# The quads of further expert blocks laid between the experts' own quads, in a kernel of two model blocks on one core

## The reference

```python
def hier_moe(h, router_g, router_g_b, router_e, router_e_b, w_gate, w_up, w_down):
    # top-1 of 4 expert groups, then top-2 of its 8 experts, gate = p(group) * renormalised p(expert | group)
    ...
    for gi in range(N_EXPERT_GROUPS):
        hid = jax.nn.silu(jnp.einsum('td,edf->tef', xt, w_gate[gi])) * jnp.einsum('td,edf->tef', xt, w_up[gi])
        hid = hid * gates[:, gi, :, None].astype(hid.dtype)
        out = out + jnp.einsum('tef,efd->td', hid, w_down[gi]).astype(f32)
```

## Time and profile before

| | us |
|---|---|
| median of 3 runs (3490.64 to 3506.99) | 3491.89 |
| the profiled execution: its own time | 3489.51 |
| the profiled execution: span from first to last instruction | 3487.7 |
| PE busy | 3098.4 |
| DVE busy | 1413.7 |
| ACT busy | 1080.6 |
| POOL busy | 310.3 |

### The profile page before, as it was taken

How to read it: one execution, slowest core, us unless ns; L and a number is a source line. 1 busy time by engine, 2 the same in 40 slices (tenths; PEclk the granted TensorE clock), 3 DMA queues, 4 the chain that set the end, 5 groups by cost and what they waited for, 6 DMA issues and landing times. The chain is left out here.

```text
span 3487.7 us, 54795 instructions
## 1 busy us (share of the span) xinstructions
PE 3098.4 (89%) x24140; PEld 2389.4 (69%) x24140; DVE 1413.7 (41%) x2665; ACT 1080.6 (31%) x1725; POOL 310.3 (9%) x460
## 2 busy tenths in 40 slices
PE   6888886888899788879999898999899998898998
PEld 5777765333788653337777676777687876777998
DVE  5455565211444641143333334333433334435554
ACT  4344443111443321133222213222332223224443
POOL 0122220111000011200000110000000000000000
PEclk9898898999999999989999899999999999999999
DMA  6333234788665169853443323453222222203452
GB/s 257 123 108 130 105 129 189 319 348 338 250 219 213 44 272 383 351 224 142 162 162 142 125 85 133 151 191 136 79 97 91 97 91 91 92 30 113 158 185 102
DMA packets 113629, 580.06 MB, mean 166 GB/s; under 512 B 24048, under 2 KB 26608, under 8 KB 60400
## 3 DMA queue, kind: packets, MB, share of 16 engines
q1 hardware_dynamic: 66160, 449.96, 34.2%
q0 software_dynamic: 47232, 126.60, 10.1%
HBM read 669.79 MB, written 1.05 MB: 192 GB/s over the span
## 5 line engine op out<-in xcount | busy, mean ns | idle before, releaser
L352 PE MATMUL ps<-t,t 128*128 128x512 f32 (+1 forms) x3488 | 1222.8, 351 | 114.3 <-DVE t L546 53.2
L353 PE MATMUL ps<-t,t 128*128 128x512 f32 (+1 forms) x3488 | 1211.7, 347 | 0.0
L354 PE MATMUL ps<-t,t 128*128 128x512 f32 (+1 forms) x3488 | 1210.2, 347 | 0.0
L329 DVE TENSOR_TENSOR t<-t,t 128x1024 fp32r<-128x1024 f32 x448 | 550.4, 1232 | 778.5 <-ACT t L310 778.4
L352 PEld LDWEIGHTS ps<-t,t 128*128 128x128 f32 x3488 | 668.2, 192 | 223.4 <-issue 69.6
L354 PEld LDWEIGHTS ps<-t,t 128*128 128x128 f32 x3488 | 668.3, 192 | 85.8
L353 PEld LDWEIGHTS ps<-t,t 128*128 128x128 f32 x3488 | 669.1, 192 | 82.0
L310 ACT ACTIVATE t<-t 128x1024 fp32r<-128x1024 f32 x448 | 469.6, 1054 | 589.1 <-PE ps L354 580.4
L1357 PE MATMUL ps<-t,t 128*32 128x512 f32 x1504 | 229.7, 638 | 46.2 <-DMA t<-in_experts_dram,t 35.9
L684 POOL DMA_DIRECT2D t<-in_wmod_dram x224 | 118.7, 535 | 1186.5 <-PE ps L633 1043.2
L1357 PEld LDWEIGHTS ps<-t,t 128*32 128x32 f32 x1504 | 52.4, 115 | 187.7 <-issue 99.4
(11 more groups left out here) (309 smaller groups left out, 2974.9 us busy)
## 6 DMA issues: line engine op xcount, KB each, us to landing
t<-in_wall_dram SPq DMA_DIRECT2D x221, 1024.0 KB
t<-in_experts_dram SPq DMA_DIRECT2D x192, 1024.0 KB, 6.5
t<-in_wmod_dram POOLq DMA_DIRECT2D x224, 512.0 KB, 5.7
t<-in_wmod_dram SPq DMA_DIRECT2D x16, 512.0 KB, 13.5
t<-in_wall_dram SPq DMA_DIRECT2D x10, 512.0 KB
t<-in_lora_dram POOLq DMA_DIRECT2D x8, 512.0 KB, 3.8
t<-in_rcst_dram POOLq DMA_DIRECT2D x1, 1536.0 KB, 6.3
t<-in_experts_dram,t POOLq DMA_INDIRECT x90, 5.6
```

The lines of the kernel that those rows point to most:

```text
L329: e.tensor_tensor(lo, self.raw(n), hi, ALU.subtract).then_inc(*net.wlo.up((self.name, n)))
L352: e.matmul(out, lh, rh, start=start, stop=False, **kw)
L353: e.matmul(out, lh, rl, start=False, stop=False, **kw)
L354: return e.matmul(out, ll, rh, start=False, stop=stop, **kw)
```

## The change

The further quads stand at turns 1, 4, 7 and 10 (`ORDER`). A method `turns` writes one list of steps, and all engines and the table of slots go by it. In each group of three turns A, O, B (O is the further quad) the steps that read weights stand as A0, O0, down of the previous B, A1, O1, B0, down A, down O, B1: two steps of the experts' own blocks stand between any two steps of the further quads, except for one at the very start. The further quads have four rooms of their own from the beginning (`far_rooms`), their own PSUM bank for gate up (3), their own gathered tokens (`Ug[1]`, gathered for two further quads at a time) and matrix `G[1]`; `hT` is doubled, and `S` has three buffers. In the first layer GpSimd clears the four rooms, which nothing has written before. The core of the diff:

```diff
-    ORDER = (0, 1, 8, 2, 3, 9, 4, 5, 10, 6, 11, 7)
+    ORDER = (0, 8, 1, 2, 9, 3, 4, 10, 5, 6, 11, 7)
...
-        self.S = [net.rview(256) for _ in range(2)]
-        self.sg, self.h, self.hT = f(256), f(256), f(256)
+        self.S = [net.rview(256), net.rview(256), net.take(256, R, at=net.nt_at + 256)]
+        self.sg, self.h, self.hT = f(256), f(256), [f(256), net.nt[0]]
...
-        first = [x for x in range(8) if net.turn[NS + x] < 0]
-        drawn = (first + [x for x in range(8) if x not in first])[0:4]
-        self.router = None
+        first = sum(net.turn[NS + x] < 0 for x in range(4, 8))
+        self.far_rooms = more[0:4]
+        net.fewer_rooms(range(4))
+        self.router, near = None, 0
...
-                if near == NS + MORE - 1:
-                    net.fewer_rooms(drawn)
                 if x >= 32:
-                    self.w[n, t, s] = net.drawn_slot(drawn[t], more[drawn[t]], ("block", x - 32, s), net.sums, key)
+                    self.w[n, t, s] = net.drawn_slot(t, more[t], ("block", x - 32, s), net.sums, key)
...
+    def turns(self):
+        out = []
+        for j in range(5):
+            A, O, B = 3 * j, 3 * j + 1, 3 * j + 2
+            if j < 4:
+                out += [("gate up", A, 0)]
+            if j == 0:
+                out += [("gather", 4, 0, 1), ("gather", 4, 1, 2)]
+            if j < 4:
+                out += [("gate up", O, 0)]
+            if j:
+                out += [("down", B - 3)]
+            if j == 4:
+                return out + [("scatter", B - 3)]
+            out += [("gate up", A, 1)]
+            if j:
+                out += [("scatter", B - 3)]
+            else:
+                out += [("gather", 4, 2, 1), ("gather", 4, 3, 2)]
+            out += [("turn", A, 0), ("gate up", O, 1), ("gate up", B, 0), ("turn", O, 3)]
+            if j < 3:
+                out += [("gather", j + 1, 0, 1), ("down", A), ("gather", j + 1, 1, 3), ("scatter", A), ("down", O), ("gate up", B, 1)]
+                out += [("scatter", O), ("turn", B, 0), ("gather", j + 1, 2, 1), ("gather", j + 1, 3, 2)]
+                if j == 1:
+                    out += [("gather", 5, kk, (3, 1, 2, 3)[kk]) for kk in range(4)]
+                continue
...
-        b = self.take(w, 0, "gate up", n) if s == 0 else self.bank("gate up", n)
+        b = self.take(w, 3 if n % 3 == 1 else 0, "gate up", n) if s == 0 else self.bank("gate up", n)
...
-        if g > 1:
-            w.wait_ge(*self.of(net.sums, "weights", 2 * g - 3, 1))
+        if g % 4:
+            w.wait_ge(*self.of(net.sums, "weights", self.members(g - 1)[1], kk // 2))
...
     def pool_blocks(self, e, w):
         net = self.net
+        if self.l == 0:
+            for x in range(4):
+                m = e.memset(self.far_rooms[x], 0.0)
+            m.then_inc(*self.up(net.pools, "rooms cleared"))
+            w.wait_ge(*self.of(net.pools, "rooms cleared"))
         w.wait_ge(*self.of(net.vecs, "block experts"))
...
-                    w.wait_ge(*marks.of(key))
+                    if freed is not None:
+                        w.wait_ge(*freed[0].of(freed[1]))
```

More of the change, by code:

```diff
@@ L830, in drawn_slot @@
         i, room = len(self.slots), NS + x
-        self.slots.append((room, ap, self.drawn[x], SW, what, self.freed[room], None))
+        self.slots.append((room, ap, self.drawn[x], SW, what, self.freed.get(room), None))
         self.drawn[x] += 1
@@ L1299, in __init__, with place, members @@
                     near += 1
-        net.fewer_rooms([x for x in range(MORE) if x not in drawn])
+        net.fewer_rooms(range(4, MORE))
         self.mods_rooms = [net.freed[NS + x] for x in range(8, MORE)]
+    def turns(self):
[23 more added lines that the diff above has]
+                    out += [("gather", 5, kk, (3, 1, 2, 3)[kk]) for kk in range(4)]
+                continue
+            pair = lambda what, x: [(what, x), (what, x + 1)] if self.ctx else []
+            out += pair("square", 0) + [("down", A)] + pair("ctx", 0) + [("scatter", A)] + pair("square", 2) + [("down", O)]
+            out += pair("ctx", 2) + [("gate up", B, 1)] + pair("square", 4) + [("scatter", O)] + pair("ctx", 4)
+            out += pair("square", 6) + [("turn", B, 0)] + pair("ctx", 6)
+    def place(self, n):
+        j, x = divmod(n, 3)
+        return (4 + j // 2, j % 2) if x == 1 else (j, x // 2)
+    def members(self, g):
+        return (3 * g, 3 * g + 2) if g < 4 else (6 * g - 23, 6 * g - 20)
     def blocks(self, n):
@@ L1447, in pe @@
         self.pe_spread(e, w)
-        for n in range(self.QUADS):
-            g, kk = n // 2 + 1, 2 * (n % 2)
-            self.pe_gate_up(e, w, n, 0)
-            if n:
-                self.pe_down(e, w, n - 1)
-            if g < 6:
-                self.pe_gather(e, w, g, kk, 3)
-            if n:
-                self.pe_scatter(e, w, n - 1)
-            if g == 6 and self.ctx:
-                for c in (2 * kk, 2 * kk + 1):
-                    self.ctx().pe_square(e, w, c)
-            self.pe_gate_up(e, w, n, 1)
-            if g < 6:
-                self.pe_gather(e, w, g, kk + 1, 1)
-            elif self.ctx:
-                for c in (2 * kk + 2, 2 * kk + 3):
-                    self.ctx().pe_square(e, w, c)
-            self.pe_turn(e, w, n, 3 if g < 6 else 0)
-        self.pe_down(e, w, self.QUADS - 1)
-        self.pe_scatter(e, w, self.QUADS - 1)
+        for what, n, *more in self.turns():
+            if what == "gate up":
+                self.pe_gate_up(e, w, n, *more)
+            elif what == "gather":
+                self.pe_gather(e, w, n, *more)
+            elif what == "turn":
+                self.pe_turn(e, w, n, *more)
+            elif what == "down":
+                self.pe_down(e, w, n)
+            elif what == "scatter":
+                self.pe_scatter(e, w, n)
+            elif what == "ctx":
+                self.ctx().pe_square(e, w, n)
         for o in range(7):
@@ L1721, in dve @@
         net.bg_dve.go(e, w, 2)
-        self.dve_choice(e, w, 1)
+        self.dve_choice(e, w, 4)
         self.dve_slots(e, w, 0)
-        for n in range(self.QUADS):
-            r = self.rows(n)
-            if n:
-                self.dve_down(e, w, n - 1)
-            w.wait_ge(*self.of(net.acts, "silu", n))
-            w.wait_ge(*self.of(net.vecs, "slot gate", n))
-            if n:
-                w.wait_ge(*self.of(net.sums, "turn", n - 1))
-            e.scalar_tensor_tensor(out=self.h[r, :], in0=self.sg[r, :], scalar=self.gs[r, n % 2:n % 2 + 1],
-                                   in1=net.ps[r, self.bank("gate up", n), 256:512], op0=ALU.mult, op1=ALU.mult).then_inc(
-                *self.up(net.vecs, "hidden", n))
-            self.emptied(net.vecs, ("hidden", n), "gate up", n)
-            if n % 2 and n < 9:
-                self.dve_choice(e, w, (n + 3) // 2)
+        for what, n, *more in self.turns():
+            if what == "down":
+                self.dve_down(e, w, n)
+            if what != "gate up" or more[0] == 0:
+                continue
+            self.dve_hidden(e, w, n)
+            if n % 3 == 0 and n < 9:
+                self.dve_choice(e, w, n // 3 + 1)
+            if n == 4:
+                self.dve_choice(e, w, 5)
             if n + 1 < self.QUADS:
                 self.dve_slots(e, w, n + 1)
-        self.dve_down(e, w, self.QUADS - 1)
         for o in range(8):
```

109 lines of the change are left out of this document (63 added, 46 removed).

## The result

| | before | changed |
|---|---|---|
| median, us | 3491.26 (4 runs, 3489.77 to 3506.99) | 3441.45 (4 runs, 3438.54 to 3446.89) |
| the profiled execution: its own time, us | 3489.51 | 3438.54 |
| first layer, first gate up step to last scatter, us | 270.3 | 243.0 |
| second layer, us | 264.9 | 244.1 |
| from the first layer's end to the second's start, us | 378.3 | 378.3 |

The ratio of the changed kernel's time to that of the kernel before is 0.9844, with a 95% interval of 0.9817 to 0.987: faster, by 1.6%. The prediction was 3439 us for the median.

What follows compares the result with a forecast made beforehand. TensorE and SyncE's fetch queue were taken to idle in turn, waiting on further fetches that move almost nothing. 3489.5 - 59.8 + 7 = 3436.7, with 2.4 to the median giving 3439 us; range 3425 to 3468.

Steps and rivals of the forecast that it cites:

- The floor by SyncE's queue: Each expert layer, if SyncE's weight fetches never stand still: 237.7 us, so 59.8 us less over both layers.
- The cost of the meeting: In each layer, two equally long chains of waits not fully hiding each other: 3.5 us per layer, 7 in all.
- The layers: Each mixture of experts, first gate up step to last scatter: 238 to 245 us for the first, against 270.3 before.
- c: Time from one further step's first fetch issue to the next one's: 19.4 us at full clock.
- the further chain: A layer's 12 further steps, each waiting for the same four rooms: 23.7 + 11c, or 237.1 us a layer.
- The further chain binds: Rival: c stays at 21.0, a layer takes 254.7 us, the whole 3466 us; chance 0.17.
- Slower: Rival: slow TensorE and deeper SyncE backlog make c 23.0, a layer 276.7 us, the whole 3510 us; chance 0.04.
- Nothing moves: Rival: another wait holds the interleaved order, time stays near 3490 us; chance 0.09 together with no gain.
- Shared bandwidth: Rival: further fetches moving bytes beside SyncE's stretch both, an estimated 323 us floor, no gain; given no chance.
- Edits at nothing: Room clearing, extra choice, doubled buffers and tail priced at nothing; at worst 1.2 us or 5.9 us, once.
- The bound of 23.7 us: GpSimd's four room clearings ahead of the first layer: at most 5.9 us each, 23.7 in all.
- The markers: Signs in the changed kernel's trace: first layer's length, DMA share, SyncE's longest wait, TensorE's block waits, and c.

Runs made afterwards that it cites:

- halves: The kernel with the lent rooms, each of the experts' own blocks fetched as two transfers of half its columns; layers 250.1 and 250.8 us, ratio 0.9899.
- the lent rooms alone: Changed kernel with the four further rooms first lent to the experts' own first four blocks, both own gate ups ahead of the first further one; ratio 0.982.
- the old steps in the new rooms: Changed kernel with its rooms, buffers and order of quads, but the step sequence of the kernel before, one step between further steps; ratio 1.0036.
- pairs: Changed kernel with further quads' steps done in two pairs of blocks and rooms given back block by block; layers 243.7 and 245.1 us, ratio 0.9793.

## Why the prediction was right, point by point

**The floor by SyncE's queue.** It was 3.64 + 5.0 + 88 x 2.52 + 7.26 = 237.7. By the timelines the first waiting block landed at 624.7, 4.9 us behind the first step's end at 619.8, and the last at 851.91 (the DMA wait shown above), and the last scatter ended 7.2 us later. The 88 distances take 227.2 us and not 221.8. 220 of them are 88 x 2.50, a little under the 2.52, and 7.2 are what six distances of 2.9 to 5.6 us have beyond that. So the term is 5.4 us short.

The run without the dropped fetches tells how much of this is theirs. Its 88 distances take 221.6 us in the first layer, so the fetches cost 5.6 of the 227.2 there and 6.2 a layer on the mean, where the prediction's terms for them came to 2.6 + 3.5 = 6.1. Without them the prediction's floor, at 2.49, is 235.0, and 237.4 and 237.2 were measured. The 2.3 us a layer by which the forecast is too short lie in that floor, in landings further apart than 2.49 us.

**The cost of the meeting.** 3.5 us a layer, a choice between 0 and 32 that no row fixed, so that it came out near is partly luck. The prediction argued that no wait of 16 us could fill all ten rooms, since two own steps lie between two further ones. At the start of a layer only one does, and there it failed. The timeline of the changed kernel:

```profile
634.29 1.89 PE L1399 MATMUL ps<-t,t 128*32 128x512 f32 x2 [3.08 <-DMA t<-in_experts_dram,t]
636.77 1.91 PE L1399 MATMUL ps<-t,t 128*32 128x512 f32 x2 [0.59 <-DMA t<-in_experts_dram,t]
639.34 1.91 PE L1399 MATMUL ps<-t,t 128*32 128x512 f32 x2 [0.66 <-DMA t<-in_experts_dram,t]
641.90 8.24 PE L1399 MATMUL ps<-t,t 128*32 128x512 f32 x58 [0.64 <-DMA t<-in_experts_dram,t]
```

O1 waits from 631.2 to 641.9 for its four fetches, B0 behind it ends at 650.1 at a granted clock of 0.50, that is 1.2 GHz, in between (the window of 634 to 644 above; TensorE had stood for 3.08 us), and the queue stops: 0.79 and 306 GB/s from 645 to 655. That is 3 us of the 7.2. The rest of them are single distances of 2.9 to 3.8 us. In the run without dropped fetches two such distances are left in each layer, of some 4.0 us; what stretches those is not known.

**The layers.** Forecast 241.2 each, measured 243.0 and 244.1: 4.7 us too little in all. The 3.2 us ahead of the first layer, which do not repeat, went the other way, so that 3436.7 met 3438.5 better than its parts did. That is luck.

**c.** Forecast 19.4, measured 19.7 and 19.5, and here the number was right and its reading only half. The prediction took c as the further chain's own length and SyncE's queue as a second chain of its own. The runs show that c is held by either: less for SyncE to fetch moves it (18.6 with 8 blocks fewer), shorter waits do not (19.2 with halves against 19.0 with the lent rooms alone), and longer ones do at once (23.1 and 21.3). The comparison with single distances of 21.0 to 23.0 in the kernel before was weak evidence too: over the ten steps its mean was 20.4 and 19.7. What was long there was not the distance but that the first further step came late and the queue stood beside it.

**The rivals.** *The further chain binds* (3466) did not come, but late by 2.6 us a step it does. *Slower* was to decide at c = 22.2; with the old steps in the new rooms c was 23.3 and 22.9, the formula 23.7 + 11c gives 280 and 275 and the layers were 278.5 and 277.4, so this rival's price is real. Its mechanism, a slow TensorE and a deeper backlog with two steps between, did not come and was not tested by itself. *Nothing moves* named the single `h` among its causes; the changed kernel keeps it, and its layers are 27 and 21 us shorter. *Shared bandwidth* with bytes stays untested: these inputs need no further block, and no run gave it any.

**Edits at nothing.** The four clearings took 7.05 us in all, from 588.42, and the first further fetch left at 611.97, 4.2 us ahead of the layer:

```profile
588.42 7.05 POOL L1812 MEMSET t<- 128x2048 f32 x4
611.97 1.07 POOL L1825 DMA_INDIRECT t<-in_experts_dram,t  x1 [16.50 <-DVE t L1634]
```

The bound of 23.7 us was three times too high. Of the 5.9 us by the rule of the Trainium skill (SBUF — State Buffer, Who interferes with whom) nothing is seen: the clearings ended 16 us before the row numbers came, and VectorE's reciprocal of 128 x 256 beside them took 1.75 us, as in the kernel before.

**The markers.** The layers (238 to 245), the DMA share (0.95 or more) and c (19 to 20.5) came as written. *SyncE's longest wait well under 29* was ill chosen, since the longest is the wait for the layer's first step. And TensorE's single waits for further blocks lie between 0.6 and 3.1 us, where 1 to 3 were forecast.

## What to carry to other kernels

A transfer that moves nothing still has to come in, and beside a full queue it takes the longer, the larger the transfers there are; so count the waits for it as steps of a chain, and give that chain's steps so much other work between them that the full queue never runs out of rooms. When two such chains have become level, a shortcut in one buys nothing (pairs, halves) and a delay costs most of its price (14 and 30 us for 29), so look for what loads both, here the dropped fetches themselves. And before a loop over blocks is turned round to free memory sooner, look whether its matmuls were sharing the array.

## What the runs showed of the hardware

- 32 matmuls with 32 output rows each, 512 columns wide, take 3.64 us when four blocks with outputs in different groups of 32 rows alternate, and 8.86 us when one block follows the other.
- An indirect fetch whose rows are all dropped takes 2.1 us where nothing else is under way, up to 13.1 us beside transfers of 1 MB (in the kernel with later further fetches), and up to 7.8 beside transfers of 512 KB (9 landings known).
- With 22 such fetches in 120 us the rate was 415 GB/s (411 in the second trace of the same kernel), and 421 without them. With the blocks fetched in transfers of 512 KB it was 403.
- A GpSimd clearing of 128 x 2048 takes 1.76 us where four follow each other, 1.8 alone, and 0.8 more pass until the next operation that waits for it (2.1 once in 22 times).
